# Opening by single tiles, the memory's two column groups in turns, and the last head pairs one slab later

## The chip, the core and the metric

One core of a Trainium2 chip runs the whole program. The metric is the device time of one execution in microseconds. Its engines are TensorE (PE; its weight loads are PEld), VectorE (DVE), ScalarE (ACT), GpSimd (POOL) and SyncE (SP, which here only issues DMAs). Each runs its own program in order and waits on semaphores.

## What is computed

Two transformer blocks in fp32 over 256 tokens of width 2048. What matters here is the first block's memory branch and the heads of its sliding window:

```
h = rmsnorm(x, norm_g);  proj = h @ w_in                       # 2048 x 11856
m_k, m_v = split(rmsnorm(mem, mem_norm_g) @ w_mem_kv)          # 256 x 2048 @ 2048 x 1024
oa = sparse_attention(...);  ob = sliding_window_attention(...);  oc = memory_attention(qc, kc, vc)
merged = g_a * (oa @ w_up_a) + g_b * (ob @ w_up_b) + g_c * (oc @ w_up_c)
x = x + merged @ w_o
# then the second block: pooling, convolution, w_o_2, an MLP of width 8192
```

## The kernel before

**Products.** Every weight matrix is streamed from HBM in slabs of 512 KB. A slab of w_mem_kv holds two row tiles (2 x 128 rows) of 512 columns. Precision comes from splitting each fp32 operand in two: ACT rounds a slab to its high half (`round_high`, L468), DVE subtracts to get the low half (`subtract_low`, L480), and TensorE makes three matmuls for each product (L605 to L607): twelve for a slab (2 row tiles x 2 token tiles x 3). The other operand is split the same way: for the memory stage `mem` is transposed on TensorE (`turn_unit`, L1345), and a unit q, which is 256 columns of `mem` turned into two row tiles of K, is scaled and rounded by ACT (`high_unit`, L831) and its remainder formed by DVE (`low_unit`, L1732), whose signal is `pair_ready`. Row tiles 2q and 2q+1 of K need unit q.

**Slabs and steps.** A `Job` (L140) lists the slabs ("pieces") of a stage; all stages form one stream of slabs. SP loads slab n into one of eight slots once the split of slab n - 8 is done (`load_slab`, L457). ACT and DVE run four slabs ahead of TensorE: in `stream` (L492) step n is, in this order, `lead(n)`, the rounding (or remainder) of slab n + 4, a body at the end of an accumulation group, and `beside(n)`. TensorE's `multiply` (L580) does slab n's products and then its own `beside(n)`. What stands in `lead` and `beside` is written by hand in tables of slab numbers.

**The memory stage** is `mem_kv`, the first job: two steps of eight slabs (columns 0 to 511 over all rows, then 512 to 1023). SP issues slabs and pieces of `mem` and `x` in an order set by `MEM_AFTER` and `X_AFTER` (L345, L346), and behind slab 9 the small parameter loads (`other_params`, L663). ACT's own queue issues `mem_norm_g` and the first 256 columns of `mem` (L816, L817). TensorE runs transposes of the identity while it has nothing else (`keep_running`, L1333), turns units 0 and 1, then starts the products. Units 2 to 7 are turned behind slabs 0 to 5 (`mem_units`, L348), and ACT and DVE make them in `lead(n)` for n = 0 to 5. ACT squares x in `beside` of steps 5 and 6, DVE takes the variance at step 7, ACT the root, DVE the reciprocal, and DVE scales x (L1771, still step 7). Behind slab 9 TensorE waits for `pair_ready` 8, which is the count of unit 7, and transposes the parameters into the PSUM bank that unit 7 used (L1368 to L1372); behind slabs 10 to 13 it turns the units of x, which need x scaled. Then `ikw` and the other jobs follow.

**Head pairs.** The heads of the three attentions are worked through beside the products of later stages. `PLACES` (L327) gives for each unit of heads the slab behind which TensorE makes its logits, the slab behind which it transposes its probabilities (L1493), and the slab behind which it weighs the values (L1520 to L1522). In `w_up_c` (4 steps of 10 slabs) stand the last three pairs of the sliding window. Transposing a pair's probabilities waits until DVE has copied out the values of the pair before (`copy_out`, L1895), since both use the same PSUM bank; DVE does that copy in its step of the same number as TensorE's values.

Of the kernel before, what the change touches and what calls it, by code (L numbers as in the profile page):

```python
# [165 lines left out]
def build(nc, A, out):  # L166
    ctx = ExitStack()
    with ctx:
# [137 lines left out]
        def column(name, k=0):  # L306
# [22 lines left out]
                  "w_up_c": (13, [(3, 10, 13), (10, 14, 17), (14, 20, 23)])}  # L329
# [78 lines left out]
        def by_rows(w, col0, slabs, lhs, ready=None):  # L408
# [5 lines left out]
            ("mem_kv", Job(2, [by_rows(A["w_mem_kv"], 0, [2] * 8, mem_pair, ("pair_ready", 0))], 2)),  # L414
# [165 lines left out]
        def multiply(pe, job, i, u, beside=None, between=None):  # L580
            for idx, (p, part, k0, kt, last) in enumerate(job.pieces):
# [13 lines left out]
                if p.ready:  # L595
                    name, before = p.ready
                    pe.wait_ge(s(name), before + ((0 if p.stride else 2 * u) + k0 + kt + 1) // 2)
                pe.wait_ge(split_done, STAGES + n + 1)
                for k in range(kt if p.rows else 0):
                    first, final = k0 + k == 0, last and k == kt - 1  # L600
# [50 lines left out]
        def _(sp):  # L651
# [24 lines left out]
            for name in names:  # L676
                job = jobs[name]
                if name == "mem_kv":
                    xr = x_of_rows
                    for n in range(2 * job.S):  # L680
                        load_slab(sp, job, 0, n // job.S, n % job.S)
                        for c, lo, hi in MEM_AFTER.get(n, ()):
                            sp.dma_start(mem_in[:, :, lo:hi], A["mem"][:, lo:hi].rearrange("(t p) d -> p t d", p=P)).then_inc(s(f"mem_in{c}"), 16)
                        if n in X_AFTER:
                            for c in X_AFTER[n]:
                                cols = slice(c * 512, (c + 1) * 512)
                                sp.dma_start(x_in[:, :, cols], xr[:, cols].rearrange("(t p) d -> p t d", p=P)).then_inc(s("x_in"), 16)
                        if n == 9:
                            other_params()
                    continue  # L690
# [118 lines left out]
        def _(act):  # L809
# [7 lines left out]
            act.dma_start(mem_in[:, :, 0:256], A["mem"][:, 0:256].rearrange("(t p) d -> p t d", p=P)).then_inc(s("mem_in0"), 16)  # L817
# [13 lines left out]
            def high_unit(pair, gain, q, first):  # L831

                act.wait_ge(s("turned_pe"), first + q + 1)
# [9 lines left out]
            for q in range(4):  # L843
                round_high(act, jobs["mem_kv"], 0, 0, q)
                if q == 0:
                    act.wait_ge(s("params_copied"), 1)
                if q < 2:
                    high_unit(mem_pair, "mem_norm_g", q, 0)

            def mem_evacuate(step, dst):  # L850
                banks, group = group_done(act, jobs["mem_kv"], 0, step)
# [7 lines left out]
            def lead_mem(n):  # L859
                for q in mem_units(n):  # L860
                    high_unit(mem_pair, "mem_norm_g", q, 0)

            def beside_mem(n):
# [8 lines left out]
                if n in (8, 9):  # L872
# [3 lines left out]
                    for c in range(5):  # L876
# [447 lines left out]
        def _(pe):  # L1324
            def products(name, beside=None, between=None):
                job = jobs[name]
                if beside:
                    for step in range(job.steps):
                        multiply(pe, job, step // job.unroll, step % job.unroll, beside, between)
# [25 lines left out]
            for q in range(2):  # L1355
                keep_running(6 if q else 11, 2)
                pe.wait_ge(s(f"mem_in{4 * q}"), 16)
                turn_unit(mem_in, q, 0)

            def beside_mem(n):  # L1360
                for q in mem_units(n):
                    if q == 3:
                        pe.wait_ge(s("params_copied"), 1)
                    if q % 2 == 0:
# [15 lines left out]
            products("mem_kv", beside_mem)  # L1380
# [298 lines left out]
        def _(dve):  # L1679
# [52 lines left out]
            def low_unit(pair, gain, q, first):  # L1732

                dve.wait_ge(s("pair_high"), 2 * (first + q) + 2)
# [7 lines left out]
            for q in range(4):  # L1742
                subtract_low(dve, jobs["mem_kv"], 0, 0, q)
                if q < 2:
                    low_unit(mem_pair, "mem_norm_g", q, 0)
# [729 lines left out]
```

## Time and profile before

| | us |
|---|---|
| median of three runs | 2054.8 (2054.5 to 2054.82) |
| the profiled execution | 2054.71 |
| its span | 2052.9 |
| busy: PE, PEld | 2040.2, 1738.2 |
| busy: DVE, ACT, POOL | 1356.1, 947.2, 81.3 |

The span is what the profiler saw between the first and the last instruction; the execution's own time is 1.8 us longer. Matmuls are busy for 99% of the span, DVE for 66% and ACT for 46%. In the page's forty equal slices the granted TensorE clock is in its highest tenth throughout, and the transfers run at 301 GB/s in the first slice and between 151 and 236 in the others but the last (106). "Idle before" an instruction is time in which its engine had nothing running, with the event that ended it.

### The profile page before, as it was taken

What the parts mean: (1) busy time and instruction counts of PE and PEld (TensorE: products, weight loads), DVE (VectorE), ACT (ScalarE), POOL (GpSimd) and SP (SyncE); (2) the same over time, 40 slices, a digit from 0 to 9 for tenths busy, and PEclk for the clock granted to TensorE, in tenths of its full rate; (3) what the DMA queues carried; (4) which work ended last, traced back from release to release, by engine and by line L of the source; (5) the groups of instructions that cost most, each with busy time, mean ns of one, the idle gap of its engine ahead of it and who ended that gap; (6) DMA issues with size and microseconds to landing.
All of it is one profiled execution on the core that took longest, in us unless ns stands there. A gap on an engine that the chain in (4) does not pass through costs nothing.

```text
span 2052.9 us, 29398 instructions
## 1 busy us (share of the span) xinstructions
PE 2040.2 (99%) x10629; PEld 1738.2 (85%) x10629; DVE 1356.1 (66%) x1811; ACT 947.2 (46%) x1223; POOL 81.3 (4%) x90
## 2 busy tenths in 40 slices
PE   9999999999999999999999999999999999999998
PEld 7888898888788888999888888888888888888886
DVE  6666766566756655578999856577557546646655
ACT  6545444565544444433444644553333333333343
POOL 0000102001002000002000000000000000000000
PEclk9999999999999999999999999999999999999999
DMA  8688555555566555555666565655565665565653
GB/s 301 195 184 196 178 155 171 193 166 180 178 206 233 187 185 187 171 175 160 194 190 198 182 234 186 205 161 183 199 190 180 199 192 181 194 194 184 194 192 106
DMA packets 265823, 387.02 MB, mean 189 GB/s; under 512 B 12411, under 2 KB 147417, under 8 KB 265180
## 3 DMA queue, kind: packets, MB, share of 16 engines
q1 hardware_dynamic: 262828, 374.83, 57.6%
q0 software_dynamic: 2576, 10.41, 2.0%
q8 instruction: 70, 1.15, 0.2%
q14 instruction: 45, 0.37, 0.1%
q10 hardware_dynamic: 304, 0.27, 0.0%
HBM read 382.79 MB, written 2.54 MB: 188 GB/s over the span
## 4 chain that ended last, share of the span: by engine, by line
PE 97%; DVE 1%; SPq 1%; DMA 1%; ACT 1%; issue 0%; DVEq 0%; ACTq 0%
PE acc L605 19%; PE acc L607 19%; PE acc L606 19%; PE acc L628 17%; PE acc L626 10%; PE acc L620 2%; PE acc L618 2%; PE acc L619 2%; PE acc L624 1%; DMA stage_rows<-in_w_mem_kv 1%; PE aux L1563 1%; PE aux L1479 1%; PE acc L548 0%; PE acc L547 0%; PE acc L546 0%
## 5 line engine op out<-in xcount | busy, mean ns | idle before, releaser
L489 DVE TENSOR_TENSOR low_rows<-stage_rows,high_rows 128x1024 fp32r<-128x1024 f32 x440 | 542.8, 1237 | 412.0 <-ACT high_rows L478 406.6
L478 ACT ACTIVATE high_rows<-stage_rows 128x1024 fp32r<-128x1024 f32 x440 | 464.6, 1059 | 583.3 <-PE acc L607 531.9
L489 DVE TENSOR_TENSOR w_low<-stage,w_high 128x1024 fp32r<-128x1024 f32 (+1 forms) x264 | 320.0, 1219 | 236.0 <-ACT w_high L478 232.3
L478 ACT ACTIVATE w_high<-stage 128x1024 fp32r<-128x1024 f32 (+1 forms) x264 | 276.2, 1047 | 420.0 <-PE acc L628 302.8
L628 PE MATMUL acc<-u,w_high 128*128 128x512 f32 x900 | 248.0, 395 | 0.0
L605 PE MATMUL acc<-high_rows,f_pair 128*128 128x512 f32 x496 | 193.2, 390 | 0.0
L606 PE MATMUL acc<-low_rows,f_pair 128*128 128x512 f32 x496 | 193.2, 389 | 0.0
L607 PE MATMUL acc<-high_rows,f_pair 128*128 128x512 f32 x496 | 193.2, 389 | 0.0
L628 PE MATMUL acc<-hT,w_high 128*128 128x512 f32 x645 | 177.5, 394 | 0.0
L628 PEld LDWEIGHTS acc<-u,w_high 128*128 128x128 f32 x900 | 153.1, 189 | 18.8
L626 PEld LDWEIGHTS acc<-u,w_low 128*128 128x128 f32 x960 | 146.9, 189 | 20.4
L626 PE MATMUL acc<-u,w_low 128*128 128x256 f32 x960 | 152.7, 281 | 0.0
L605 PE MATMUL acc<-high_rows,hT 128*128 128x512 f32 x384 | 151.9, 396 | 0.0
L607 PE MATMUL acc<-high_rows,hT 128*128 128x512 f32 x384 | 149.8, 390 | 0.0
L606 PE MATMUL acc<-low_rows,hT 128*128 128x512 f32 x384 | 149.8, 390 | 0.0
L628 PEld LDWEIGHTS acc<-hT,w_high 128*128 128x128 f32 x645 | 109.8, 189 | 13.3
L626 PEld LDWEIGHTS acc<-hT,w_low 128*128 128x128 f32 x688 | 104.1, 189 | 15.5 <-issue 2.6
L626 PE MATMUL acc<-hT,w_low 128*128 128x256 f32 x688 | 112.1, 285 | 0.0
L618 PE MATMUL acc<-uT,w_high 128*128 128x272 f32 x384 | 111.3, 290 | 0.0
L620 PE MATMUL acc<-uT,w_high 128*128 128x272 f32 x384 | 111.0, 289 | 0.0
L619 PE MATMUL acc<-uT,w_low 128*128 128x272 f32 x384 | 110.5, 288 | 0.0
L605 PEld LDWEIGHTS acc<-high_rows,f_pair 128*128 128x128 f32 x496 | 93.2, 188 | 19.3
(414 smaller groups left out, 3356.5 us busy)
## 6 DMA issues: line engine op xcount, KB each, us to landing
stage_rows<-in_w_in SPq DMA_DIRECT2D x160, 512.0 KB, 3.6
stage<-in_w_in SPq DMA_DIRECT2D x136, 512.0 KB, 3.5
stage_rows<-in_w_down SPq DMA_DIRECT2D x128, 512.0 KB, 4.3
stage<-in_w_up SPq DMA_DIRECT2D x120, 512.0 KB, 3.8
stage_rows<-in_w_o SPq DMA_DIRECT2D x64, 512.0 KB, 3.6
stage_rows<-in_w_mem_kv SPq DMA_DIRECT2D x16, 512.0 KB, 9.0
stage_rows<-in_w_pool_out SPq DMA_DIRECT2D x16, 512.0 KB, 4.1
stage_rows<-in_w_conv_out SPq DMA_DIRECT2D x16, 512.0 KB, 4.5
```

Source lines behind the costliest of these rows:

```text
L478: act.activation(high[:, pr, 0:kt, 0:p.cols], src[:, slot, 0:kt, 0:p.cols], ACT.Copy).then_inc(high_done, 1)
L489: dve.tensor_tensor(low[:, pr, 0:kt, 0:p.cols], src[:, slot, 0:kt, 0:p.cols], high[:, pr, 0:kt, 0:p.cols].bitcast(F32), ALU.subtract).then ...
L605: pe.matmul(bk, x_high, high, start=first, stop=False)
L606: pe.matmul(bk, x_high, low, start=False, stop=False)
L607: mm = pe.matmul(bk, x_low, high, start=False, stop=final)
L618: pe.matmul(dst, tile(w_high, k), b, start=first, stop=False)
L619: pe.matmul(dst, tile(w_low, k), a, start=False, stop=False)
L620: mm = pe.matmul(dst, tile(w_high, k), a, start=False, stop=final)
L624: pe.matmul(bk, tile(w_high, 0), p.rhs(0)[0], start=True, stop=False, skip_group_check=True)
L626: pe.matmul(bk[:, 0:T], tile(w_low, k), p.rhs(k0 + k)[1], start=False, stop=False, skip_group_check=True)
L628: mm = pe.matmul(bk, tile(w_high, k), p.rhs(k0 + k)[0], start=False, stop=last and k == kt - 1, skip_group_check=True)
L1479: mm = pe.matmul(aux[:, logits_bank(h), lo:hi], q[:, t * P:(t + 1) * P], k[:, 0:hi - lo], start=True, stop=True)
```

## The change

Three edits. The first slab and the first 256 columns of `mem` are loaded as single row tiles, alternating, all on SP's queue; ACT, DVE and TensorE treat them tile by tile (`first_in`, `first_unit`, `first_products`). `mem_kv` becomes one step with two column groups as parts, whose slabs alternate while the row tile is below 8 (`in_turns=8`): row tiles 0-1 of group 0, then of group 1, then 2-3 of group 0, and so on for eight slabs; then row tiles 8 to 15 of group 0 and of group 1. The units of `mem` follow `MEM_TURN_AT`: unit 1 is turned behind slab 0, unit 2 behind slab 2, unit 3 behind slab 4, units 4 to 7 behind slabs 5 to 8, and ACT and DVE make them in `lead` of the same numbers. And in `w_up_c` the second pair's transposes and values and all three places of the third pair come one slab later.

```diff
@@ class Job @@
-    def __init__(self, steps, parts, unroll, by_tile=0):
+    def __init__(self, steps, parts, unroll, by_tile=0, in_turns=0):
...
+        if in_turns:
+            self.pieces.sort(key=lambda piece: (piece[2], piece[1]) if piece[2] < in_turns else (in_turns + piece[1], piece[2]))
@@ tables @@
-                  "w_up_c": (13, [(3, 10, 13), (10, 14, 17), (14, 20, 23)])}
+                  "w_up_c": (13, [(3, 10, 13), (10, 15, 18), (15, 21, 24)])}
-        MEM_AFTER = {1: [(4, 256, 512)], 2: [(1, 512, 1024)], 3: [(2, 1024, 1536)], 5: [(3, 1536, 2048)]}
+        MEM_AFTER = {1: [(4, 256, 512)], 3: [(1, 512, 1024)], 4: [(2, 1024, 1536)], 5: [(3, 1536, 2048)]}
+        MEM_TURN_AT = {0: 1, 2: 2, 4: 3, 5: 4, 6: 5, 7: 6, 8: 7}
-        def mem_units(n):
-            return (n + 2,) if n < 6 else ()
-            ("mem_kv", Job(2, [by_rows(A["w_mem_kv"], 0, [2] * 8, mem_pair, ("pair_ready", 0))], 2)),
+            ("mem_kv", Job(1, [by_rows(A["w_mem_kv"], c * ROW, [2] * 8, mem_pair, ("pair_ready", 0)) for c in range(2)], 1, in_turns=8)),
@@ SP @@
-                    for n in range(2 * job.S):
-                        load_slab(sp, job, 0, n // job.S, n % job.S)
+                    for n in range(job.S):
+                        if n == 0:
+                            for k in range(2):
+                                sp.dma_start(mem_in[:, :, k * P:(k + 1) * P], ...).then_inc(s("mem_in5" if k else "mem_in0"), 16)
+                                sp.dma_start(stage_rows[:, 0, k, :], A["w_mem_kv"][k * P:(k + 1) * P, 0:ROW]).then_inc(s("first_in") if k == 0 else landed[0], 16)
+                            sp.sem_inc(issued, 1)
+                        else:
+                            load_slab(sp, job, 0, 0, n)
@@ ACT @@
-            act.dma_start(mem_in[:, :, 0:256], ...).then_inc(s("mem_in0"), 16)
-            for q in range(4):
+            act.wait_ge(s("first_in"), 16)
+            act.activation(high_rows[:, 0, 0, :], stage_rows[:, 0, 0, :], ACT.Copy).then_inc(s("pair_high"), 1)
+            act.wait_ge(s("params_copied"), 1)
+            act.wait_ge(s("turned_pe"), 1)
+            act.activation(mem_pair[:, 0, 0, :], aux[:, 0, 0:T], ACT.Copy, scale=column("mem_norm_g", 0)).then_inc(s("pair_high"), 1)
+            act.wait_ge(landed[0], 16)
+            act.activation(high_rows[:, 0, 1, :], stage_rows[:, 0, 1, :], ACT.Copy).then_inc(high_done, 1)
+            act.wait_ge(s("turned_pe"), 2)
+            act.activation(mem_pair[:, 1, 0, :], aux[:, 3, 0:T], ACT.Copy, scale=column("mem_norm_g", 1)).then_inc(s("pair_high"), 1)
+            for q in range(1, 4):
                 round_high(act, jobs["mem_kv"], 0, 0, q)
...
+                if q == 1:
+                    high_unit(mem_pair, "mem_norm_g", 1, 0)
             def lead_mem(n):
-                for q in mem_units(n):
-                    high_unit(mem_pair, "mem_norm_g", q, 0)
+                if n and n in MEM_TURN_AT:
+                    high_unit(mem_pair, "mem_norm_g", MEM_TURN_AT[n], 0)
@@ TensorE @@
-            for q in range(2):
-                keep_running(6 if q else 11, 2)
-                pe.wait_ge(s(f"mem_in{4 * q}"), 16)
-                turn_unit(mem_in, q, 0)
+            for k in range(2):
+                keep_running(1 if k else 3, 2)
+                pe.wait_ge(s("mem_in5" if k else "mem_in0"), 16)
...
+                for t in range(2):
+                    mm = pe.transpose(aux[:, 3 * k, t * P:(t + 1) * P], mem_in[:, t, k * P:(k + 1) * P], ident[:])
+                mm.then_inc(s("turned_pe"), 1)
+            keep_running(2, 2)
+            def first_products(k):
+                if k == 0:
+                    pe.wait_ge(s("first_unit"), 2)
+                    return
+                pe.wait_ge(split_done, STAGES + 1)
+                pe.wait_ge(s("pair_ready"), 1)
             def beside_mem(n):
-                for q in mem_units(n):
+                q = MEM_TURN_AT.get(n)
+                if q is not None:
...
@@ DVE @@
-            for q in range(4):
+            for k in range(2):
...
+                dve.tensor_tensor(low_rows[:, 0, k, :], stage_rows[:, 0, k, :], high_rows[:, 0, k, :].bitcast(F32), ALU.subtract).then_inc(s("first_unit") if k == 0 else split_done, 1)
+                dve.wait_ge(s("pair_high"), k + 2)
+                dve.scalar_tensor_tensor(out=mem_pair[:, k, 1, :], ...).then_inc(s("first_unit") if k == 0 else s("pair_ready"), 1)
+            for q in range(1, 4):
                 subtract_low(dve, jobs["mem_kv"], 0, 0, q)
-                if q < 2:
-                    low_unit(mem_pair, "mem_norm_g", q, 0)
+                if q == 1:
+                    low_unit(mem_pair, "mem_norm_g", 1, 0)
             def lead_mem(n):
-                for q in mem_units(n):
-                    low_unit(mem_pair, "mem_norm_g", q, 0)
+                if n and n in MEM_TURN_AT:
+                    low_unit(mem_pair, "mem_norm_g", MEM_TURN_AT[n], 0)
```

## Rows read from the trace of the kernel before

**Rows 1.** The page: span; engine, busy us (share of span) xinstructions.
```profile
span 2052.9 us, 29398 instructions
PE 2040.2 (99%) x10629; PEld 1738.2 (85%) x10629; DVE 1356.1 (66%) x1811; ACT 947.2 (46%) x1223; POOL 81.3 (4%) x90
```
**Rows 2.** Waits of TensorE, whole span: total us, times, longest.
```profile
PE aux L1336 <- POOLq L707: 2.0, 1, 2.0
PE aux L1493 <- DVE late L1895: 1.4, 1, 1.4
...
PE acc L605 <- DVEq L1740: 0.7, 1, 0.7
```
**Rows 3.** Order of time, opening: start, us, instruction, [idle before <-releaser].
```profile
3.43 2.41 PE L1336 MATMUL aux<-ident 128*128 128x128 f32 x11
...
5.33 1.06 ACT L478 ACTIVATE high_rows<-stage_rows 128x1024 fp32r<-128x1024 f32 x1 [2.16 <-DMA stage_rows<-in_w_mem_kv]
...
6.09 0.66 PE L1352 MATMUL aux<-ident,mem_in 128*128 128x128 f32 x4 [0.25 <-DMA mem_in<-in_mem]
...
8.75 0.47 PE L605 MATMUL acc<-high_rows,mem_pair 128*128 128x512 f32 x1
...
11.95 0.48 PE L605 MATMUL acc<-high_rows,mem_pair 128*128 128x512 f32 x1
```
**Rows 4.** Groups by form, 0 to 70 us: busy us, mean ns, idle before.
```profile
L489 DVE TENSOR_TENSOR low_rows<-stage_rows,high_rows 128x1024 fp32r<-128x1024 f32 x16 | 19.5, 1225 | 14.4 <-ACT high_rows L478 13.7
L478 ACT ACTIVATE high_rows<-stage_rows 128x1024 fp32r<-128x1024 f32 x16 | 16.9, 1055 | 10.2 <-DMA stage_rows<-in_w_mem_kv 10.2
...
L1737 DVE SCALAR_TENSOR_TENSOR mem_pair<-aux,params,mem_pair 128x256 fp32r<-128x256 f32 x16 | 7.0, 478 | 0.8 <-ACT mem_pair L836 0.8
L836 ACT ACTIVATE mem_pair<-aux,params 128x256 fp32r<-128x256 f32 x16 | 6.6, 466 | 2.7 <-PE aux L1352 2.7
...
L489 DVE TENSOR_TENSOR w_low<-stage,w_high 128x512 fp32r<-128x512 f32 x4 | 2.8, 692 | 2.3 <-ACT w_high L478 1.8
L478 ACT ACTIVATE w_high<-stage 128x512 fp32r<-128x512 f32 x4 | 2.5, 632 | 4.3 <-PE acc L607 4.3
```
**Rows 5.** Order of time, slab 7 and slabs 10 to 11.
```profile
24.47 1.06 ACT L478 ACTIVATE high_rows<-stage_rows 128x1024 fp32r<-128x1024 f32 x1 [1.51 <-DMA stage_rows<-in_w_mem_kv]
...
34.40 1.06 ACT L478 ACTIVATE high_rows<-stage_rows 128x1024 fp32r<-128x1024 f32 x1 [1.04 <-DMA stage_rows<-in_w_mem_kv]
35.37 1.90 ACT L839 ACTIVATE junk<-x_in 128x2048 f32<-128x2048 f32 x1
...
38.34 1.23 DVE L489 TENSOR_TENSOR low_rows<-stage_rows,high_rows 128x1024 fp32r<-128x1024 f32 x1 [1.61 <-ACT high_rows L478]
...
39.73 0.20 ACT L829 ACTIVATE rs<-rs 128x2 f32<-128x2 f32 x1 [1.43 <-DVEq L1717]
...
40.26 0.45 PE L1371 MATMUL aux<-ident,prow 90*128 90x90 f32 x3
40.28 2.48 DVE L1771 TENSOR_SCALAR x_in<-x_in,rs 128x2048 f32<-128x2048 f32 x2
```
**Rows 6.** Order of time, SP's issues of slabs 10 to 15.
```profile
28.10 3.43 SPq L466 DMA_DIRECT2D stage_rows<-in_w_mem_kv  x6
```
**Rows 7.** Order of time, w_up_c behind slab 14.
```profile
535.12 1.23 DVE L489 TENSOR_TENSOR low_rows<-stage_rows,high_rows 128x1024 fp32r<-128x1024 f32 x1
536.26 0.42 DVE L1895 COPY late<-aux 128x256 f32<-128x256 f32 x1
...
536.82 0.84 PE L1493 MATMUL aux<-ident,lg_bc 128*128 128x128 f32 x6 [1.38 <-DVE late L1895]
```
**Rows 8.** Transfers from 19 to 24 us: queue, packets, MB, share of 16 engines.
```profile
q1 hardware_dynamic: 1001, 1.92, 104.2%
q8 instruction: 1, 0.02, 1.4%
```
**Rows 9.** The page, DMA issues: KB each, median us from issue to landing.
```profile
stage_rows<-in_w_in SPq DMA_DIRECT2D x160, 512.0 KB, 3.6
```

More of the change, by code:

```diff
@@ L578, in first_by_tile, with multiply @@
                     between(t, idx)
-        def multiply(pe, job, i, u, beside=None, between=None):
+        def multiply(pe, job, i, u, beside=None, between=None, first_slab=None):
             for idx, (p, part, k0, kt, last) in enumerate(job.pieces):
@@ L594, in multiply @@
                 pr = n_static % PAIRS
-                if p.ready:
+                by_k = first_slab if idx == 0 else None
+                if p.ready and not by_k:
                     name, before = p.ready
                     pe.wait_ge(s(name), before + ((0 if p.stride else 2 * u) + k0 + kt + 1) // 2)
-                pe.wait_ge(split_done, STAGES + n + 1)
+                if not by_k:
+                    pe.wait_ge(split_done, STAGES + n + 1)
                 for k in range(kt if p.rows else 0):
+                    if by_k:
+                        by_k(k)
                     first, final = k0 + k == 0, last and k == kt - 1
@@ L831, in high_unit @@
             def high_unit(pair, gain, q, first):
-                act.wait_ge(s("turned_pe"), first + q + 1)
+                act.wait_ge(s("turned_pe"), first + q + 2)
                 for a in range(2):
@@ L842, in _ @@
             act.activation(rs[:, 0:1], ones[:, 0:1], ACT.Sqrt)
-            for q in range(4):
+            act.wait_ge(s("first_in"), 16)
[8 more added lines that the diff above has]
+            for q in range(1, 4):
                 round_high(act, jobs["mem_kv"], 0, 0, q)
-                if q == 0:
-                    act.wait_ge(s("params_copied"), 1)
-                if q < 2:
-                    high_unit(mem_pair, "mem_norm_g", q, 0)
+                if q == 1:
+                    high_unit(mem_pair, "mem_norm_g", 1, 0)
             def mem_evacuate(step, dst):
-                banks, group = group_done(act, jobs["mem_kv"], 0, step)
+                banks, group = group_done(act, jobs["mem_kv"], 0, 0, step)
                 act.wait_ge(s("chain_done"), 2)
@@ L875, in beside_mem @@
                         act.wait_ge(s("input_squared"), 3)
-                    for c in range(5):
+                    for c in range(6):
                         act.wait_ge(s(f"mem_in{c}"), 16)
@@ L1324, in _, with products @@
         def _(pe):
-            def products(name, beside=None, between=None):
+            def products(name, beside=None, between=None, first=None):
                 job = jobs[name]
@@ L1328, in products @@
                     for step in range(job.steps):
-                        multiply(pe, job, step // job.unroll, step % job.unroll, beside, between)
+                        multiply(pe, job, step // job.unroll, step % job.unroll, beside, between, None if step else first)
                     return
@@ L1379, in beside_mem @@
                         turn_unit(x_in, q, 8)
-            products("mem_kv", beside_mem)
+            products("mem_kv", beside_mem, first=first_products)
             products("ikw")
@@ L1732, in low_unit @@
             def low_unit(pair, gain, q, first):
-                dve.wait_ge(s("pair_high"), 2 * (first + q) + 2)
+                dve.wait_ge(s("pair_high"), 2 * (first + q) + 3)
                 for a in range(2):
@@ L1740, in low_unit @@
                 dve.sem_inc(s("pair_ready"), 1)
-            for q in range(4):
+            for k in range(2):
+                if k == 0:
+                    dve.wait_ge(s("pair_high"), 1)
+                else:
+                    dve.wait_ge(high_done, 1)
+                dve.tensor_tensor(low_rows[:, 0, k, :], stage_rows[:, 0, k, :], high_rows[:, 0, k, :].bitcast(F32), ALU.subtract).then_inc(s("first_unit") if k == 0 else split_done, 1)
+                dve.wait_ge(s("pair_high"), k + 2)
+                dve.scalar_tensor_tensor(out=mem_pair[:, k, 1, :], in0=aux[:, 3 * k, 0:T], scalar=column("mem_norm_g", k),
+                                         in1=mem_pair[:, k, 0, :].bitcast(F32), op0=ALU.mult, op1=ALU.subtract).then_inc(s("first_unit") if k == 0 else s("pair_ready"), 1)
+            for q in range(1, 4):
                 subtract_low(dve, jobs["mem_kv"], 0, 0, q)
-                if q < 2:
-                    low_unit(mem_pair, "mem_norm_g", q, 0)
+                if q == 1:
+                    low_unit(mem_pair, "mem_norm_g", 1, 0)
             def splitting(name, body, links=0, beside=None, at_once=False):
```

10 lines of the change are left out of this document (5 added, 5 removed).

## The prediction

> **What bounds the kernel now.** I read the page first, then TensorE's waits, then the opening in order of time. Matmuls fill 99% of the span [rows 1], so work of the other engines is free until TensorE waits for it, and TensorE waits in few places: 2.0 us at the very start, 0.7 us in the memory stage for a signal of VectorE, 1.4 us near 536 us for VectorE's copy [rows 2]. Apart from these the order of the products is a queue without holes from 8.75 us on. So the change can win only (a) what lies ahead of the first product at 8.75 us, (b) those 0.7 us, (c) those 1.4 us; and any new wait of TensorE is paid in full at the end, for nothing behind the memory stage has slack on TensorE. The largest possible gain is about 2.4 + 0.7 + 1.4 = 4.5 us.
>
> The profiled execution took 2054.71 us, its span 2052.9; the median of the runs is 2054.8. I add to 2054.71 and quote the result for the median, 0.1 us apart.
>
> **The opening.** Before, the first slab (512 KB) is rounded from 5.33 us, and the first product starts at 8.75 [rows 3]. Now the slab comes as two tiles of 256 KB, each behind a 128 KB tile of `mem`, and one queue carries them: 128 + 256 KB stand ahead of the first rounding where 512 KB of slab and part of a second queue's 256 KB stood. I put the landing of the first tile at 4.5 us, an estimate from 5.3 us for the whole slab. Then: rounding of 512 elements 0.63, its remainder 0.69, the remainder of the mem tile 0.48 (its high half, 0.47, lies beside the 0.69) [rows 4], hand-overs 0.1: first product at 6.4 us, 2.35 us earlier. Bounds: 0 (TensorE waits for the second mem tile and the whole slab as before) to 3.0. Since ACT's queue loses one DMA and SP gets three where it had one, SP issues 0.5 to 1.3 us later at first; the transfers ahead of it are as many bytes, so from the second slab on landings stay where they were. The shorter run of `keep_running` (11 instead of 22 transposes) can leave TensorE slow for longer: before, 11 transposes at 3.43 us took 2.41 us, 0.22 each, and four at 6.09 took 0.66, 0.11 apart [rows 3]. If the slow pace holds through the first slab, that costs 1.4 us. None of these decide, as follows.
>
> **The turns.** Slabs go column group 0, 1, 0, 1, ... over row tiles 0 to 7, and only then the rest. A unit (two row tiles of mem, transposed, scaled, split) is so needed every second slab, and the units are placed later: unit 3 in step 4, units 4 to 7 in steps 5 to 8; before, units 2 to 7 in steps 0 to 5. What counts is who stands ahead of them in the in-order queues of ACT and DVE.
>
> Unit 3 is needed by slab 6 (rows 6 and 7 of K). Its high half on ACT stands behind the rounding of slab 7, which starts only when that slab has landed, 24.47 us [rows 5]; the transfers fill the DMA engines there (104% of 16 for the one queue [rows 8]), and no byte ahead of slab 7 goes away. High half at 25.4 to 26.3, the slab's remainder on DVE to 26.8, the low half 0.87 more: ready at 27.6. TensorE gets there at about 26.0: slab 0 from 6.4, a slab with a unit 3.2 us (8.75 to 11.95 [rows 3]), one without 2.8, small waits of 0.2, 0.4 and 0.2 us at slabs 1, 2 and 4 whose halves end on DVE at 9.8, 13.0 and 19.4. It waits 1.6 us, and slab 6 starts at 27.7 where it had started at 28.25. The opening's gain is nearly gone here.
>
> **The wait that takes over.** Unit 7 was done in step 5, ahead of everything that x needs. Now it is in step 8, and TensorE waits for it before the parameter transposes of step 9 (`pair_ready` 8), with slab 10, the turns of x and the whole rest of the kernel behind that wait. ACT's and DVE's work up to it is a chain tied not to TensorE but to slab 10's landing: SP issues slabs 10 to 15 only behind the small parameter loads, at 28.10 [rows 6], and ACT starts on slab 10 at 34.40. Neither is touched by the change. From there, with the rows of before [rows 5] and what is put in:
> - ACT: slab 10 at 34.40, square of x at 35.37, 1.90 long, to 37.3. New: unit 6, 0.82, to 38.1 (unit 5's, one step ahead, fits into the 1.0 us in which ACT idled before 34.40). Slab 11 to 39.1.
> - DVE: remainder of slab 11, 38.34 before, now 39.16 to 40.4. Then variance, root (39.73 before, now 40.55), reciprocal, and the scaling of x, 40.28 before, now 41.1, 2.48 long: to 43.6. Unit 6's low half fits into the idle 1.6 us ahead of slab 11.
> - New behind the scaling: unit 7's low half, two of 0.48 less overlap, 0.87: to 44.4. Its high half runs on ACT meanwhile. Signal and start 0.1: TensorE goes on at 44.5.
>
> Before, TensorE was at these transposes at 40.26. So it is 44.5 - 40.26 = 4.2 us late, whatever it had won till then: it would arrive at about 40.3 and idle 4 us. The 0.7 us of the old wait are within this. Behind it the transposes of x find x scaled, slabs 11 to 15 are issued in one go behind slab 10 [rows 6], and the tail of the stage runs at TensorE's pace as before; ACT's evacuation of the first group stands in the same step. So nothing is given back. Bounds of this term: +4.2, with unit 6 partly hidden +3.4, and +2.1 if slab 10 comes earlier (rivals).
>
> **The last head pairs.** DVE copies pair 13's values out at 536.26, behind the remainder at 535.12; TensorE, done with slab 14, waits 1.38 us for it [rows 7]. One slab later means 2.8 us later on TensorE, and the copy ends at 536.7: the wait is covered. Issues that move: six transposes, eight logits products, ACT's copy and exponentials, DVE's logits; the third pair's scaling falls into step 17 beside a gate group and its copy out of the second pair into 18, one slab ahead of what follows as before; DVE has three slabs of lead there. Value -1.38, bounds -1.4 and +0.5 (another late copy).
>
> **Sum.** 2054.71 + 4.2 - 1.4 = 2057.5 us, and 2057.5 for the median too.
>
> **Rivals.**
> - *Slab 10 comes earlier* (13%). From its issue at 28.10 to ACT's start on it lie 6.3 us [rows 5, 6], where w_in's slabs take 3.6 [rows 9]; around 22 us one instruction fetch sits among the transfers [rows 8], and a slab has landed only when its last part has. If that fetch is what delays it and falls elsewhere, slab 10 lands at 28.1 + 0.6 (one issue of six in 3.43) + 3.6 = 32.3, 2.1 us earlier, the chain too: 2054.7 + 2.1 - 1.4 = 2055.4. Against: the fetch belongs to a point of a program that hardly shifts.
> - *The clock falls in the new hole* (8%; the other side). TensorE idles about 4 us at 40 us, longer than anywhere in the trace. If it comes back at the slow pace of the opening (0.22 against 0.11 per transpose), and stays there as long as it did from 1.96 to 5.4 us [rows 2, 3], half of 3.5 us is lost: +1.7, 2059.2. It decides from the hole's length; a slower first slab shortens it. The Trainium skill ("TensorE: Matmul & The Clock Gate", section "HAM oscillation — how this bites in real kernels") says that a wait between bursts of matmuls puts the engine back to half clock and each such wait pays the warm-up anew; by that rule the sum is 2059.2, by the rows it is open, for the trace has no hole of this length behind the opening.
> - *The head pairs' wait only moves* (13%): 2054.7 + 4.2 = 2058.9. For: DVE is what was late. Against: a slab of slack.
> - *The opening's gain survives* (4%): the walk above is wrong, unit 7 is not late, and all three terms are won: 2054.7 - 2.35 - 0.7 - 1.4 = 2050.3.
> - The forecast, 62%.
>
> **How the numbers follow.** 0.2% is 4.1 us, about what can be told from no change: faster means below 2050.7, slower above 2058.9. Faster 0.04 (the last rival). Slower: the clock 0.08, half of the head pairs' 0.13, and 0.03 for a hole longer than I reckon, 0.17. Same 0.79. Range 2055.0 to 2059.2: it holds the early slab 10, the forecast and the head pairs' case, and leaves out the surviving gain and the half of the clock's.
>
> **What would show it.** A wait of TensorE at the transposes of the parameters (L1371's successor) for DVE, about 4 us, ending near 44.5; the first product near 6.4; a wait of about 1.6 us at slab 6 for unit 3; DVE's scaling of x starting near 41.1 with two SCALAR_TENSOR_TENSOR of mem_pair behind it; no wait at L1493's successor. The prediction is wrong if TensorE reaches the second half of the memory stage without waiting for unit 7, or if ACT starts on slab 10 well before 34 us.

## The result, and the profile after

| | before | after |
|---|---|---|
| median of 8 runs each, us | 2054.77 (2054.5 to 2055.02) | 2061.26 (2059.4 to 2062.35) |
| ratio | | 1.0032, 95% interval 1.0021 to 1.0042 |
| profiled execution, its span, us | 2054.71, 2052.9 | 2062.35, 2060.6 |

The change makes the kernel 6.5 us slower. The forecast was 2057.5, the range ended at 2059.2. The profiled execution of after is the slowest of its eight; I compare profile with profile and median with median.

The page of after, to [rows 1]: TensorE is busy for 1.9 us more, of a span that is 7.7 us longer.

```profile
span 2060.6 us, 29381 instructions
PE 2042.1 (99%) x10618; PEld 1737.6 (84%) x10618; DVE 1356.5 (66%) x1812; ACT 947.5 (46%) x1224; POOL 81.4 (4%) x90
```

TensorE's waits of after in the first 62 us (what it waited for, us in total, times, longest), to [rows 2]. The large one, in front of the parameter transposes (L1399, before L1371), is for DVE's signal of a finished unit (L1768). The 2.0 us at the very start stood in before as well, and so did waits for `mem` (1.0 us in two pieces there). The three in front of products (1.0, 0.7, 0.4) take the place of one of 0.7, and the 1.4 us of [rows 2] are gone.

```profile
PE aux L1399 <- DVEq L1768: 5.5, 1, 5.5
PE aux L1351 <- POOLq L716: 2.0, 1, 2.0
PE acc L608 <- DVEq L1768: 1.0, 1, 1.0
PE aux L1367 <- DMA mem_in<-in_mem: 0.9, 1, 0.9
PE acc L608 <- DVE low_rows L488: 0.7, 1, 0.7
PE acc L608 <- DVE mem_pair L1777: 0.4, 1, 0.4
```

The opening of after in order of time, to [rows 3] (ACT, then TensorE, then ACT's and DVE's work on slab 1). The first product starts at 6.29, not 8.75. Slab 1 is rounded from 9.79, where it was 7.57 before, and TensorE, done with slab 0 at about 10.0, stands until 12.25 but for one turn.

```profile
4.31 0.63 ACT L852 ACTIVATE high_rows<-stage_rows 128x512 fp32r<-128x512 f32 x1 [1.56 <-DMA stage_rows<-in_w_mem_kv]
...
6.29 0.77 PE L608 MATMUL acc<-high_rows,mem_pair 128*128 128x512 f32 x1 [0.43 <-DVE mem_pair L1777]
...
9.59 0.40 PE L610 MATMUL acc<-high_rows,mem_pair 128*128 128x512 f32 x1
10.87 0.66 PE L1367 MATMUL aux<-ident,mem_in 128*128 128x128 f32 x4 [0.88 <-DMA mem_in<-in_mem]
12.25 0.47 PE L608 MATMUL acc<-high_rows,mem_pair 128*128 128x512 f32 x1 [0.72 <-DVE low_rows L488]
...
9.79 1.06 ACT L477 ACTIVATE high_rows<-stage_rows 128x1024 fp32r<-128x1024 f32 x1 [2.47 <-DMA stage_rows<-in_w_mem_kv]
```

The transfers from 4 to 9 us, of before and of after (packets, MB, mean rate). In the same five microseconds 0.62 MB less arrive, which is 1.6 us at the 389 GB/s of the five that follow.

```profile
DMA packets 1230, 1.83 MB, mean 367 GB/s; under 512 B 79, under 2 KB 591, under 8 KB 1230
```
```profile
DMA packets 778, 1.21 MB, mean 243 GB/s; under 512 B 50, under 2 KB 303, under 8 KB 778
```

The chain up to unit 7 in after, to [rows 5, 6]: SP's issue of slabs 10 to 15, ACT from slab 10, DVE, TensorE. Read it by the starts: issue 28.10 before, now 30.08; slab 10 rounded at 34.40 before, now 37.09; x scaled at 40.28 before, now 43.78; behind it unit 7's low half; TensorE goes on at 47.16, where it was at 40.26. Of the 2.7 us by which slab 10 is later, 2.0 are SP's issue of it; the other 0.7 lie between issue and landing.

```profile
30.08 4.18 SPq L465 DMA_DIRECT2D stage_rows<-in_w_mem_kv  x6
...
37.09 1.06 ACT L477 ACTIVATE high_rows<-stage_rows 128x1024 fp32r<-128x1024 f32 x1 [1.90 <-DMA stage_rows<-in_w_mem_kv]
38.05 1.90 ACT L847 ACTIVATE junk<-x_in 128x2048 f32<-128x2048 f32 x1
...
39.95 0.82 ACT L844 ACTIVATE mem_pair<-aux,params 128x256 fp32r<-128x256 f32 x2
...
41.83 1.23 DVE L488 TENSOR_TENSOR low_rows<-stage_rows,high_rows 128x1024 fp32r<-128x1024 f32 x1
...
43.78 2.48 DVE L1808 TENSOR_SCALAR x_in<-x_in,rs 128x2048 f32<-128x2048 f32 x2
46.17 0.87 DVE L1765 SCALAR_TENSOR_TENSOR mem_pair<-aux,params,mem_pair 128x256 fp32r<-128x256 f32 x2
...
47.16 0.83 PE L1399 MATMUL aux<-ident,prow 90*128 90x90 f32 x3 [5.55 <-DVEq L1768]
```

The last step is in the table by stage of after (stretch, length, busy us of each engine, granted clock, DMA). "The hole" is the 5.55 us in front of 47.16. Right behind it the granted clock is at half (1.2 GHz); from 52.2 on it is whole again (2.4 GHz). In order of time a matmul there takes 0.63, later 0.39.

```profile
45.40:52.10 6.70, 4.94 (x14) 3.69 (x15) 5.12 (x12) 4.43 (x5) 0.00 (x0) 0.50 0.33 101
52.20:60.00 7.80, 7.80 (x44) 6.59 (x43) 5.04 (x9) 5.04 (x10) 0.00 (x0) 1.00 0.38 119
```
```profile
51.64 0.63 PE L610 MATMUL acc<-high_rows,mem_pair 128*128 128x512 f32 x1
...
52.34 0.39 PE L609 MATMUL acc<-low_rows,mem_pair 128*128 128x512 f32 x1
```

The sum over these rows: resumed 47.16 - 40.26 = 6.9 us late; from 47.16 to 52.1 at half clock, half of 4.9 lost, 2.5; the head pairs -1.4: +8.0, where the two profiled executions differ by 7.64; the sum is 0.4 too large.

### The profile page after: what moved, and what is told of

Its sections match the earlier page's. It is cut to its first block, busy times and chain, and to the rows that moved or that the text cites. A ratio compares the mean times of both kernels' runs of the same rounds, so it can differ in the third digit from the quotient of the medians.

```text
span 2060.6 us, 29381 instructions
## 1 busy us (share of the span) xinstructions
PE 2042.1 (99%) x10618; PEld 1737.6 (84%) x10618; DVE 1356.5 (66%) x1812; ACT 947.5 (46%) x1224; POOL 81.4 (4%) x90
## 4 chain that ended last, share of the span: by engine, by line
PE 97%; SPq 1%; DVE 0%; DMA 0%; issue 0%; ACT 0%; DVEq 0%
PE acc L608 19%; PE acc L610 19%; PE acc L609 19%; PE acc L631 17%; PE acc L629 10%; PE acc L623 2%; PE acc L621 2%; PE acc L622 2%; PE acc L627 1%; PE aux L1507 1%; PE aux L1591 1%; PE aux L1521 0%; PE acc L547 0%; PE acc L545 0%; SPq L465 0%; PE acc L546 0%
```

## The experiments

Three theories stood. **A, unit 7:** TensorE stands behind slab 9 because unit 7's low half is queued behind x's scaling on DVE. **B, the landings:** the new opening makes the slabs land later, and that is the loss. **C, the clock:** the hole itself is cheap, the half clock behind it is not. The kernel before was timed again beside every group of experiments, with medians of 2054.77 to 2054.86, so medians of different groups are compared as they stand.

**pairs_only**: the kernel before and this line of the change alone.

```
-                  "w_up_c": (13, [(3, 10, 13), (10, 14, 17), (14, 20, 23)])}
+                  "w_up_c": (13, [(3, 10, 13), (10, 15, 18), (15, 21, 24)])}
```


> The kernel before with the head-pair edit alone. If the 1.38 us wait near 536 us is covered by one slab, 2054.8 - 1.4 = 2053.4 us and no wait for the copy-out of late is left; if the wait only moves, 2054.8.

Measured 2053.29 (2052.97 to 2053.67), ratio 0.9993 (0.9983 to 1.0003): 1.5 us under before in the medians, with no overlap of the runs, and no wait for the copy in the trace. This part did what it was put down for.

**turns_only**: the turns, the later units and the later pieces of memory, with the old opening and the old head places.

```
+        MEM_TURN_AT = {2: 2, 4: 3, 5: 4, 6: 5, 7: 6, 8: 7}
-            return (n + 2,) if n < 6 else ()
+            return (MEM_TURN_AT[n],) if n in MEM_TURN_AT else ()
```


> The kernel before with the turns, the later units and the later mem pieces, but with its own opening (whole first slab, first mem piece on ACT's queue) and the old head places. Theory (the chain of x holds unit 7 back): slab 10 lands at 34.4 as before, TensorE waits behind slab 9 until 44.5 us, 4.2 us late: 2059.0 us, and 1.7 to 2.5 more if the clock falls in the hole. Rival (the single-tile opening makes the loss, the turns alone are free): 2054.8 or a little less.

Measured 2061.36 (2060.62 to 2062.48), ratio 1.0033 (1.0021 to 1.0046). Its trace is the prediction's chain nearly to the tenth: slab 10 rounded at 34.61, x scaled from 41.29 (41.1 forecast), TensorE back at 44.67 (44.5 forecast). The rows below are of TensorE and of DVE in order of time.

```profile
44.67 0.83 PE L1374 MATMUL aux<-ident,prow 90*128 90x90 f32 x3 [5.04 <-DVEq L1743]
...
41.29 2.48 DVE L1774 TENSOR_SCALAR x_in<-x_in,rs 128x2048 f32<-128x2048 f32 x2
43.69 0.87 DVE L1740 SCALAR_TENSOR_TENSOR mem_pair<-aux,params,mem_pair 128x256 fp32r<-128x256 f32 x2
```

Where the forecast has +4.2, this kernel has +6.5: the granted clock is 0.50 from 44 to 47 us and 0.80 on the mean of 47 to 52.

```profile
44.00:47.00 3.00, 2.33 (x7) 1.69 (x8) 2.85 (x5) 3.00 (x4) 0.00 (x0) 0.50 0.00 0
47.00:52.00 5.00, 5.00 (x23) 4.14 (x22) 1.73 (x9) 2.07 (x6) 0.00 (x0) 0.80 0.69 215
```

**fill_hole**: the changed kernel, with TensorE busy on transposes of the identity in the hole.

```
                 if n == 9:
+                    keep_running(50, 1)
                     pe.wait_ge(s("pair_ready"), 8)
```


> The changed kernel with 50 transposes of the identity (0.11 us each, 5.5 in all) ahead of the wait behind slab 9, so that TensorE is not idle there. Theory (5 us at half the clock behind the hole cost 2.5): granted clock 1.0 behind 47 us, 2061.3 - 2.5 = 2058.8 us. Rival (the clock's fall costs nothing that a later wait would not have taken): 2061.3.

Measured 2059.73 (2059.24 to 2060.2), 1.5 us under after in the medians, 2.4 between the profiled executions. TensorE goes on as late as in after (46.87, was 47.16), but at the whole clock, from the three rows of transposes and products onward. The whole clock alone gives back what the sum above put down for it, 2.4 of 2.5 us between the profiled executions, and the rest of the loss stays: C is a part and only a part.

```profile
41.17 5.62 PE L1351 MATMUL aux<-ident 128*128 128x128 f32 x50
46.87 0.51 PE L1400 MATMUL aux<-ident,prow 90*128 90x90 f32 x3
...
47.44 0.50 PE L608 MATMUL acc<-high_rows,mem_pair 128*128 128x512 f32 x1
```

**two_queues**: the changed kernel, with the two single tiles of `mem` issued by ACT in its own queue.

```
+            for k in range(2):
+                act.dma_start(mem_in[:, :, k * P:(k + 1) * P], ...).then_inc(s("mem_in5" if k else "mem_in0"), 16)
```


> The changed kernel with the two 128-column pieces of mem on ACT's DMA queue, the slab's tiles on SP's. Theory (one queue for all small pieces slows the transfers between 4 and 9 us, 200 to 290 GB/s against 350 to 400, and delays slab 10 from 34.4 to 37.1 us): slab 10 lands near 34.4 again, TensorE goes on near 44.5 instead of 47.2, 2058.5 us. Rival (it is the tiles, not the queue): slab 10 stays at 37, 2061.3.

Measured 2061.15 (2060.93 to 2061.86). The first product is at 8.33, so the opening's gain is gone; slab 10 is rounded at 35.63, 1.5 us sooner than in after and 1.0 later than in turns_only; from 4 to 9 us 1.29 MB arrive. Nothing is won in time: TensorE goes on at 45.69, but at half clock up to 51.45, which is 5.8 us of work.

**units_sooner**: the changed kernel, units 3 to 7 one slab sooner.

```
-        MEM_TURN_AT = {0: 1, 2: 2, 4: 3, 5: 4, 6: 5, 7: 6, 8: 7}
+        MEM_TURN_AT = {0: 1, 2: 2, 3: 3, 4: 4, 5: 5, 6: 6, 7: 7}
```


> The changed kernel with units 3 to 7 turned and rounded one slab sooner each, so that DVE's part of unit 7 stands ahead of its scaling of x and not behind it. Theory (TensorE stands still behind slab 9 because unit 7 is queued behind x's scaling): in the changed kernel's trace x is scaled at 43.78 and 45.0, ready at 46.2, so that the wait behind slab 9 (5.5 us) goes and one of about 1.3 us for x stays behind slab 10; the granted clock stays at 1.0 up to 52 us, which gives back 2.5 more. Time 2061.3 - 4.2 - 2.5 = 2054.6. Rival (the late landing of slab 10 holds TensorE whatever the order of the units): a wait of 4 us or more stays, and the time is 2060 or over.

Measured 2055.58 (2054.71 to 2056.49), ratio to before 1.0004 (0.9995 to 1.0014): 5.7 us under after with the same opening and the same loads. TensorE passes the parameter transposes at 40.13 without a wait, waits 0.94 us for x behind slab 10, and the clock stays whole. This decides for A as the larger part. One thing differs besides the edit: slab 10 is rounded at 35.42 in this execution and at 37.09 in that of after. A pair without that difference is turns_only and whole_sooner below (old opening, slab 10 at 34.61 and 34.42). Less 1.5 for the head pairs, turns_only is 5.8 us over whole_sooner in the medians: the same size. Units 3 to 6 moved with unit 7, but it is the wait for unit 7 that is gone.

```profile
40.13 0.50 PE L1399 MATMUL aux<-ident,prow 90*128 90x90 f32 x3
...
44.64 1.09 PE L1367 MATMUL aux<-ident,x_in 128*128 128x128 f32 x8 [0.94 <-DVE x_in L1808]
```

**params_pool**: the changed kernel, with the small parameter loads (24 DMAs, which the expectation counts as 27) moved from SP's queue to POOL's.

```
-                        if n == 9:
-                            other_params()          # SP
+            other_params()                          # POOL, behind its constants
```


> The changed kernel with the 27 small loads of parameters issued by POOL in its own queue at the opening, and no longer by SP ahead of slabs 10 to 15. Theory (the chain that ends in unit 7 hangs on the landing of slab 10): SP issues slab 10 at 21 to 24 us and not at 30.08, it lands at 28 to 33 and not at 37.07, x's scaling starts 4 us or more sooner (43.78 before), the wait behind slab 9 shrinks from 5.5 to under 1.5 us, the clock stays at 1.0. Time 2061.3 - 4.5 - 2.5 = 2054.3. Rival (the transfers are held by the bytes in front of them, not by their issue): slab 10 lands at 36 or later, wait and time as in the changed kernel, 2061. Second rival: the small loads collide with the opening's tiles, and the first product (6.29) is a microsecond or more later.

Measured 2061.19 (2060.48 to 2061.92): the expectation failed. Slab 10 does land sooner (its last part at 33.24, 37.07 in after), and x is scaled at 42.45, only 1.3 us sooner than in after. ACT's rows show why: from slab 8's landing, at 30.54, it works with no idle time to 40.4, and DVE's variance waits for that work.

```profile
30.54 1.06 ACT L477 ACTIVATE high_rows<-stage_rows 128x1024 fp32r<-128x1024 f32 x1 [2.54 <-DMA stage_rows<-in_w_mem_kv]
31.50 0.82 ACT L846 ACTIVATE mem_pair<-aux,params 128x256 fp32r<-128x256 f32 x2
32.21 1.06 ACT L477 ACTIVATE high_rows<-stage_rows 128x1024 fp32r<-128x1024 f32 x1
33.16 1.91 ACT L849 ACTIVATE junk<-x_in 128x2048 f32<-128x2048 f32 x1
...
35.77 1.07 ACT L477 ACTIVATE high_rows<-stage_rows 128x1024 fp32r<-128x1024 f32 x1
36.72 1.93 ACT L849 ACTIVATE junk<-x_in 128x2048 f32<-128x2048 f32 x1
...
39.32 1.08 ACT L477 ACTIVATE high_rows<-stage_rows 128x1024 fp32r<-128x1024 f32 x1
```

So the chain has a second root: slab 8's landing and the 11.9 us from its rounding to x's scaling (12.0 in units_sooner, where ACT has no idle time either). By this count, an estimate, an early slab 10 lets x be scaled 2.0 us sooner in after (slab 8 rounded at 29.84) and 0.7 in turns_only (28.67), and no more; here only 1.3 came of it, since slab 8 itself was 0.7 later. The wait of 3.7 us that stays still brings the half clock.

**whole_one_queue**: turns_only, with the first piece of memory ahead of slab 0 in SP's queue.

```
-            act.dma_start(mem_in[:, :, 0:256], ...).then_inc(s("mem_in0"), 16)
+                        if n == 0:
+                            sp.dma_start(mem_in[:, :, 0:256], ...).then_inc(s("mem_in0"), 16)
```


> The kernel before with the column groups in turns and the units later (as turns_only), and the first piece of memory (columns 0 to 255) ahead of slab 0 in SP's queue and not in ACT's; slab 0 and this piece stay whole. It parts the two things that the opening changed in the transfers. If the single queue makes the slow transfers of 5 to 9 us: GB/s falls to about 250 in these slices as in the changed kernel, slab 10 lands at 36 or later (34.6 in turns_only), TensorE resumes at 46 or later, time 2062 to 2063. If the single tiles make them: slab 10 lands at 34.6, and the time is that of turns_only, 2061.4.

Measured 2062.87 (2061.99 to 2063.66, four runs), 1.5 us over turns_only in the medians, 0.8 in the profiled executions; the runs of the two overlap. Slab 10 is rounded at 35.27 (34.61 there); from 4 to 9 us 1.42 MB arrive (1.77 there). So one queue seems to cost without any single tile, half as much in slab 10's landing as expected and as much in time.

**turns_pairs**: the kernel before with the turns and the head pairs, the units and the pieces of memory where they were.


> The kernel before with the column groups in turns alone (the units of memory and its pieces where they were, unit 7 in the lead of slab 5, ahead of x's scaling) and with the head pairs one slab on. Theory (the turns cost nothing, the later units do): no wait behind slab 9, x is waited for behind slab 10 as before, clock 1.0; time as with the head pairs alone, 2053.3 (2052.8 to 2053.8). Rival (turns cost by themselves, since the group of the first columns ends six slabs later and its evacuation moves): 2054.5 or over.

Measured 2053.12 (2052.66 to 2053.88), ratio 0.9992 (0.9983 to 1.0001), as pairs_only (2053.29). In sum the turns cost nothing. In the profiled executions they win 0.8 us up to slab 15 (the wait for unit 7 is gone) and lose 0.3 behind it. There the first product of the next job (L627) waits for PSUM banks that ACT frees when it has copied out the first column group. That copy waits for memory's scale from DVE, and starts only 0.6 us sooner than in pairs_only (59.11, there 59.69).

```profile
59.11 1.27 ACT L858 ACTIVATE mk_rows<-acc,rs 128x512 f32<-128x512 f32 x2 [0.96 <-DVEq L1727]
60.48 0.50 PE L627 MATMUL acc<-hT,w_high 128*128 128x512 f32 x1 [0.34 <-ACTq L860]
```

**whole_sooner** and **tiles_early** fill up a table of two by two. whole_sooner has the units and pieces of memory exactly as units_sooner, and the old opening. tiles_early has the opening by tiles and the units early; they stand one slab behind those of turns_pairs (unit 7 in step 6, not 5), since the opening leaves unit 1 to step 0, so its expectation says a little too much with "that they had before".


> The kernel before with the turns, the head pairs one slab on and units 3 to 7 at the places that they have in units_sooner (unit 7 in the lead of slab 7), and with the old opening: what parts it from units_sooner is the opening by single tiles alone. Theory A (the opening costs time, since slabs 8 and 9 and with them the squares of x come later): x is scaled by 42.6 as in turns_pairs (44.5 in units_sooner), slab 11's products end near 46.2 (48.1), time 2053.1 to 2053.6, 2 to 2.5 under units_sooner. Theory B (the later places of the units make what is left of the loss, the opening nothing): 2055.5, as units_sooner.

> The changed kernel with the units at the places that they had before (unit 3 in the lead of slab 2, unit 7 in that of slab 6) and the pieces of memory behind slabs 1, 2, 3 and 5: the opening by single tiles is all that parts it from turns_pairs. Theory A (the end of this stage is the scaling of x and 3.6 us, whatever TensorE gained before): the wait in front of slab 4 (0.8) goes and slab 9 ends a microsecond sooner, but x is scaled at 44.5 again and slab 11 ends at 48.1: 2055.5, as units_sooner. Theory B (the products themselves end the stage, and the gain of the opening comes through once the units are in time): slab 11 ends at 45.5 or sooner, 2052.5.

| median, us (turns and pairs in all) | units early | unit 7 in step 7, as units_sooner |
|---|---|---|
| old opening | 2053.12 (turns_pairs) | 2054.00 (2053.72 to 2055.37, whole_sooner) |
| opening by tiles | 2054.69 (2053.7 to 2056.53, tiles_early) | 2055.58 (units_sooner) |

Across a row: the later units and pieces of memory cost 0.9 us in the medians (two steps above, one step below; in the lower row the two profiled executions, 2055.09 and 2054.83, don't show it). Down the second column the opening is all that differs, and costs 1.6 us; the first column gives 1.6 too, with the units one step later in the lower kernel. A third pair has unit 7 late: turns_only less 1.5 for the head pairs is 2059.9, after 2061.3, so 1.4. whole_sooner's theory A was right in kind and too large (2 to 2.5 us expected). That of tiles_early has the wait for x right and the median 0.8 us too high (2055.5 expected). Both theories B are out.

**tiles_early_x** and **turns_pairs_x**: tiles_early and turns_pairs, with the squares of x, the variance and the root one slab sooner.

```
-                if n in (5, 6):        # ACT: squares of x
+                if n in (4, 5):
-                if n == 7:             # ACT: root; DVE: variance, reciprocal, x's scaling
+                if n == 6:
```


> tiles_early with the chain to x's scale one slab sooner on ScalarE and VectorE (the squares of x behind the rounding of slabs 8 and 9, the root behind slab 10's). Theory A (x's scale is the anchor): x is scaled 2 to 3 us sooner than in tiles_early (44.5 expected there), by 42; TensorE doesn't wait for x, slab 11 ends 2 us sooner or more, time 2 us or more under tiles_early, so 2053.5 or less, and under turns_pairs (2053.1) only if the opening's gain is then kept. Rival: the squares hold back the rounding of slab 9 and unit 5, TensorE waits there for 2 us, and nothing is gained.

> turns_pairs (old opening) with the same move of x's chain. TensorE waited for x by a few tenths there (slab 10 ends 42.19, slab 11 3.97 later, where 3.6 is the rule), so theory A gives 0.3 to 0.4 less, 2052.7; the rival, that the rounding of slab 9 comes too late, 2054 or more.

tiles_early_x: 2053.24 (2052.68 to 2053.77), 1.45 under tiles_early. turns_pairs_x: **2052.39** (2051.94 to 2052.53), ratio 0.9988 (0.9979 to 0.9997), which beats before by 2.4 us and after by 8.9. In tiles_early TensorE waited 1.3 us for x (first row below). tiles_early_x ends slab 15 2.3 us sooner, and loses 0.5 of it again behind slab 15, where TensorE now waits 0.9 us for ACT's copy at L627 (second row). In turns_pairs_x no wait over 0.4 us is left behind the start (the rest); yet its slab 15 is no sooner than in turns_pairs, since its products began 0.4 us later (9.24, there 8.84), about what the vanished wait for x gives. Its 0.6 us in the profiled executions lie behind slab 15: ACT's copy starts at 58.11 without a wait, not at 59.11. The expectation had the time nearly right (2052.7), but not the place where it is won.

```profile
PE aux L1367 <- DVE x_in L1808: 1.3, 1, 1.3
PE acc L627 <- ACTq L872: 0.9, 1, 0.9
```
```profile
PE aux L1339 <- POOLq L710: 2.0, 1, 2.0
PE acc L608 <- issue: 0.4, 1, 0.4
PE aux L1346 <- DMA prow<-in_mem_norm_g: 0.2, 1, 0.2
```

All kernels in one table. "x ready" is the start of DVE's scaling of x and its 2.48 us; "slab 15" the start of its last product; "behind" the profiled time less that.

| kernel | median | x ready | slab 15 | behind |
|---|---|---|---|---|
| before | 2054.8 | 42.8 | 60.6 | 1994.1 |
| turns_only | 2061.4 | 43.8 | 67.1 | 1994.1 |
| whole_one_queue | 2062.9 | 44.4 | 68.0 | 1994.0 |
| pairs_only | 2053.3 | 43.2 | 60.6 | 1992.9 |
| after | 2061.3 | 46.3 | 69.8 | 1992.6 |
| two_queues | 2061.2 | 44.8 | 68.7 | 1992.4 |
| params_pool | 2061.2 | 44.9 | 68.8 | 1992.5 |
| fill_hole | 2059.7 | 46.0 | 67.3 | 1992.6 |
| units_sooner | 2055.6 | 44.6 | 61.7 | 1993.1 |
| tiles_early | 2054.7 | 44.8 | 62.0 | 1993.1 |
| whole_sooner | 2054.0 | 43.6 | 60.7 | 1993.2 |
| turns_pairs | 2053.1 | 42.6 | 59.8 | 1993.2 |
| tiles_early_x | 2053.2 | 42.1 | 59.6 | 1993.6 |
| turns_pairs_x | 2052.4 | 40.5 | 59.8 | 1992.6 |

The last column has two levels, 1994.1 with the old head places and 1992.4 to 1993.6 with the new. The 1.2 us within the second arise within 12 us behind slab 15, at the product that needs ACT's copy: 1992.4 to 1992.6 where it has no wait, 1993.1 to 1993.2 with a wait of 0.3, 1993.6 with one of 0.9. (In pairs_only, 1992.9, it starts 0.46 us behind slab 15's last product, in before 0.23.) Where x comes sooner, a part of the gain goes there. The first product, which the opening moves by 2.5 us, shows in no column. With the turns, and with unit 7 ahead of x's scaling, the last product of slab 15 starts 17.1 us behind "x ready" in four kernels (turns_pairs, whole_sooner, units_sooner, tiles_early); in turns_pairs_x it is 19.3, and there TensorE's own pace from its first product on ends the stage. So an earlier first product can count only in a kernel like that one. tiles_early_x is such a kernel with a first product 2.3 us sooner (6.89), and its slab 15 is 0.2 sooner.

## Why the prediction was wrong, step by step

- **First product at 6.4:** 6.29. Right. But the trace's first record of a whole clock begins at 7.76, within slab 0 (the matmuls take 0.63 before and 0.40 after it); in before it begins at 5.5, ahead of the first product. In the other kernels with single tiles that moment lies between 7.0 (units_sooner) and 11.8 (fill_hole, whose slab 0 ends at 12.1, later than the 11.8 of before). With whole first tiles it always lies ahead of the first product (5.5 to 8.0, the product at 8.7 or later; 9.4 and 9.7 in whole_one_queue). The prediction had named 1.4 us for this and put it at nothing; in after it was 1.5 us of work at half clock, so 0.7.
- **"From the second slab on landings stay where they were":** wrong, the first failed step. Slab 1 was rounded 2.2 us later, slab 10 2.7 us later. It counted bytes and SP's issue times and took the rate for fixed; the rate fell by a third from 4 to 9 us. By the table of two by two this and all else of the opening cost 1.6 us (1.4 with unit 7 late); the forecast had put it at nothing. In the profiled executions, of which after's is its slowest, it moved TensorE's return from 44.7 (turns_only) to 47.2. Why the transfers were slower stays open.
- **Unit 3's wait of 1.6 us at slab 6:** about 0.4 (slab 6 ends 3.56 us behind slab 5, where 3.2 is the pace). The prediction's terms give 25.6 for TensorE's arrival there, not 26.0, and let it arrive with its gain from the opening; the gain was spent at slab 1 already, and on 1.0 us for unit 2 in front of slab 4.
- **The wait that takes over:** right in place, cause and size where the landings are as before (turns_only: 44.67 against 44.5), and shown by units_sooner, which takes unit 7 out from behind x's scaling and gets 5.7 us back. The anchor was half right: slab 10's landing, with slab 8's 0.7 us behind it in turns_only, so that the rival of an early slab 10 could have given back about 0.7 us, not 2.1 (an estimate from the 11.9 us of params_pool).
- **The clock in the new hole:** taken as a rival at 8% and 1.7 us; it happened in every kernel here with a wait of 3.7 us or more in that place (after, turns_only, whole_one_queue, two_queues, params_pool) and in none with 1.3 us or less. It cost 2.2 us in turns_only (4.3 us of work at half clock), 2.5 in after, 2.9 at most (two_queues). That is the second failed step, and the larger: the term was put at nothing in the sum and at 8% among the rivals, though "the trace has no hole of this length" speaks for no side. The page that it cited, "TensorE: Matmul & The Clock Gate" of the Trainium skill, section "HAM oscillation — how this bites in real kernels", holds that a wait between bursts of matmuls puts the engine back to half clock. This case agrees: the granted clock is 0.50 behind the hole.
- **Head pairs -1.4:** -1.5. Right.

The kernels form a chain from before to after, one part at each step, in medians: head pairs -1.5 (pairs_only), turns -0.2 (turns_pairs), units 3 to 7 and the pieces of memory later but unit 7 still ahead of x's scaling +0.9 (whole_sooner), opening +1.6 (units_sooner), and unit 7 behind x's scaling, with the clock, +5.7 (after): +6.5 in all. Such a chain adds up by construction. What supports the sizes is that the opening (1.6, 1.6, 1.4) and the last step (5.7, 5.8) come out alike from pairs of kernels off the chain. The forecast had -1.4 and +4.2; the 3.8 us that it lacked are the clock (2.2 to 2.5) and the opening (1.4 to 1.6).

## What to carry to other kernels

Before an operation is moved to a later step of an in-order queue, list what stands ahead of it there and what waits for its signal; here a unit of 0.87 us moved behind 2.5 us of scaling cost 5.7, the half clock behind the wait included. An earlier first product is worth nothing where the stage ends on a chain that hangs on transfers: shorten that chain first (ACT's squares one slab sooner gave 0.7 to 1.5 us), look at what waits next behind it, and see that the opening doesn't make its loads late. Where a forecast has TensorE stand still in one piece for as long as here (3.7 to 5.5 us, five kernels of five), put the half clock behind it (2.2 to 2.9 us here) into the sum, not among the rivals.

## What was not expected of the hardware

- **The opening's order of DMAs changes the rate of what follows.** From 4 to 9 us 1.83 MB arrive in before, 1.77 in turns_only, 1.42 with memory's first piece in SP's queue (whole_one_queue), 1.29 with single tiles on two queues, 1.21 in after. From 9 to 14 us these move 1.94 to 2.00 MB. That it goes with the opening is shown by all fourteen executions: the six kernels with the old one have 1.67 to 1.83 MB, the six with single tiles on one queue 1.17 to 1.32. The Trainium skill ("DMA: Bandwidth & Descriptors", section "Issuing engines are not separate DMA queues") holds that issuing on several engines saves only the issuing time. SP's issue of that piece takes 0.45 us, and the move cost 1.5 us in the medians (2062.87 of four runs against 2061.36 of six, with runs that overlap), which speaks against the rule without settling it. The cause is open: the figures for the queue alone and for two queues are of one profiled execution each, and whether it is the queue, the order of the first transfers or their sizes was not parted further.
- **Slab 10's landing differs among kernels with the same opening.** ACT starts on it at 37.09 in after, 36.81 in fill_hole, 36.47 in tiles_early and 35.42 in units_sooner, and the runs of these kernels spread over 1.0 to 3.0 us, those of before over 0.5 (8 runs) to 1.1 (23 runs). A slab is there with the last of its sixteen parts: in after those of slab 1 landed from 6.4 to 9.8 us, the last 1.6 behind the one before it; in before all landed within 0.5 us, by 7.4. Of slab 10 the last part can straggle by itself: in fill_hole it landed at 36.79, 2.35 us behind the one before it, in before 2.26 behind (34.38), in units_sooner the last two came together at 35.4.
- **The opening by single tiles comes to its products at half clock**, for 1.5 us in after and for 0.8 (units_sooner) to 4.9 us (fill_hole) in the others. It runs fewer transposes ahead of them and starts them sooner; which of the two does it was not parted.
- **Half a clock outlasts its cause.** Behind the hole of after, TensorE worked without a pause from 47.16, and the clock was back only at 52.1.
